# Third up projection of a transformer block pair: 19 of 22 gate/value pairs as seven products of quarter matrices, weight sums by accumulating DMAs

## The chip, the cores and the metric

One core of one Trainium2 chip. The metric is the device time of one launch in microseconds; the kernel before has 1698.54 us as the median of 3 runs (1698.29 to 1701.11). All inputs lie in device memory in float32.

## The reference

512 tokens of width 1024 go through a block with a pooling mixer and a convolutional feed-forward, then through two more blocks: forgetting attention with a SwiGLU feed-forward, and an S5 state-space mixer with a SwiGLU feed-forward. The change touches the last of these feed-forwards:

```python
D_FF_2 = 2816
def swiglu(h, w_gate, w_up, w_down):
    return (jax.nn.silu(h @ w_gate) * (h @ w_up)) @ w_down
# last lines of second_block
h = rmsnorm(x, ffn_pre_gain[i])
x = x + rmsnorm(swiglu(h, ffn_w_gate[i], ffn_w_up[i], ffn_w_down[i]), ffn_post_gain[i])
```

Here h is 512 x 1024, the two up matrices are 1024 x 2816 each, the down matrix 2816 x 1024.

## The kernel before

The stages run one after the other on TensorE: start-up and pooling, first up and down projection (`S_UP1`, `S_DN1`), attention, second up and down (`S_UP2`, `S_DN2`), S5 mixer (`S_S5I`, `S_GLU`, `S_S5O`), third up (`S_UP3`) and third down (`S_DN3`). Every float32 operand is split into a high float32r part and the rest, and a product is three passes (`passes`, L2013 to L2016): high by high, low activation by high weight, high activation by low weight.

Weights come as numbered slots through a ring of five buffers `raw`. SP issues the load of slot n when slot n - 5 is through TensorE (`ring_free`, which waits on `slot_mm`); ScalarE makes `w_hi` from it (`hi`, L806); VectorE subtracts and writes `w_lo` (`lo`, L1235); both do so three slots ahead of TensorE (`LEAD = 3`). SP, ScalarE, VectorE and GpSimd each work off their own list in order, so a wait in a list holds all that is behind it.

The third up projection has 44 slots, a gate tile and a value tile in turn. A slot is 8 blocks of 128 rows times three passes of 512 tokens. ScalarE takes Silu of the gate bank (L915), VectorE multiplies by the value bank (L1409) into `a11_s1` or `a12_a22`, and after each second pair makes the sums `s1`, `s2`, `s3`, `s4` (L1411 to L1421) that the third down projection uses: that stage is already done as seven products of quarter matrices in place of eight (`down_products`), with 11 blocks in a product and two slots' worth of banks.

The weights of that down projection need sums of quarters of `dn3`. GpSimd makes them in device memory with 32 DMAs (`weight_sums`, L1993), copies and accumulating ones, one after the other: step t waits for slot `start + t` on TensorE and for the landing of step t - 1. They start at `S_UP2 + 2`. Before them in GpSimd's list stand `s5_parameters` and the 16 `turn_tables`; each of these waits for SP's store of the one before, and SP stores them between the attention's loads (L688). After them stand the eight subtractions `hl` (L2009) that the S5 stage's gate matrix needs.

In the S5 stage ScalarE evicts a bank (`evict_u`, L1142), writes it to `u_scratch` by DMA (L1144), waits for the landing and reads it back in another order into `ub` (L1150), eight times, and only then goes on in its list; TensorE waits for `ub` at L2447.

## Time and profile before

| | |
|---|---|
| median of 3 runs | 1698.54 us |
| the profiled execution | 1701.21 us |
| its span, first to last instruction | 1699.4 us |
| granted TensorE clock, mean | 0.984 |
| TensorE busy | 1636.5 us (96%) |
| VectorE, ScalarE, GpSimd busy | 1019.0, 679.4, 267.5 us |

The profiled execution is 2.7 us above the median, and 1.8 us of it lie outside the span. TensorE's busy time counts overlapping matmuls once; the spacing of starts in its timeline tells what one costs. PEld is the load of the stationary operand, which runs beside the matmuls.

### The profile page before, as it was taken

Reading aid. Unit: us, or ns where it says so; the run is one execution under the profiler, and the core shown is the slowest. Engines: PE = TensorE matmul, PEld = TensorE weight load, DVE = VectorE, ACT = ScalarE, POOL = GpSimd, SP = SyncE. Lnnn points to the kernel's source line nnn. Section 1 sums busy time; section 2 is a strip of 40 time slices with the busy share of each in tenths; the row PEclk is TensorE's granted clock in tenths of the full one; section 3 lists DMA queues with packets and bytes.
Section 4 is the critical chain, followed back from the end, with each engine's and each line's share of the span. In section 5 each row is a group of like instructions: output and inputs, shape, how many; then the busy total and the mean of one; then the engine's idle time right before and its main releaser. Section 6 shows DMA issues by size and latency. Waiting matters only on the chain.

```text
span 1699.4 us, 21739 instructions
## 1 busy us (share of the span) xinstructions
PE 1636.5 (96%) x8385; PEld 1355.5 (80%) x8385; DVE 1019.0 (60%) x1645; ACT 679.4 (40%) x1078; POOL 267.5 (16%) x777
## 2 busy tenths in 40 slices
PE   6489999999999999999999999999999999999997
PEld 5478888888877787778888888888878888888886
DVE  6988666686554776756333337667727633333576
ACT  4455433323344767754222222333225522222564
POOL 2011700000017777730110100000010000000000
PEclk8789999999999999999999999999999999999999
DMA  8923233334342222225787763467853223232564
GB/s 351 384 76 100 87 100 99 98 126 138 98 120 84 69 76 65 85 81 169 212 197 210 211 163 126 137 191 229 261 157 125 92 98 99 100 99 88 167 190 144
DMA packets 150521, 242.30 MB, mean 143 GB/s; under 512 B 29601, under 2 KB 112913, under 8 KB 147090
## 3 DMA queue, kind: packets, MB, share of 16 engines
q1 hardware_dynamic: 130898, 210.49, 38.8%
q0 software_dynamic: 4608, 23.07, 6.0%
q10 hardware_dynamic: 14912, 7.34, 1.6%
q8 instruction: 67, 1.10, 0.3%
q14 instruction: 36, 0.29, 0.1%
HBM read 223.05 MB, written 40.89 MB: 155 GB/s over the span
## 4 chain that ended last, share of the span: by engine, by line
PE 86%; DVE 6%; DMA 4%; ACT 2%; issue 1%; POOL 0%; ACTq 0%; DVEq 0%; SPq 0%
PE bank L2014 26%; PE bank L2015 26%; PE bank L2016 26%; DVE ada L1338 2%; DMA u_scratch<-us 1%; PE bank L2328 1%; PE bank L2301 1%; PE bank L2146 1%; DVE htok L1322 1%; PE bank L2457 1%; DMA raw<-in_fox_in 1%; PE bank L2054 1%; DVE w_lo L1235 1%; ACT junk_h L874 1%; DVE xt L1298 1%
## 5 line engine op out<-in xcount | busy, mean ns | idle before, releaser
L2014 PE MATMUL bank<-hh,w_hi 128*128 128x512 f32 (+1 forms) x1440 | 552.7, 384 | 5.2 <-POOL hl L2009 3.3
L2015 PE MATMUL bank<-hl,w_hi 128*128 128x512 f32 (+1 forms) x1440 | 549.2, 381 | 0.0
L2016 PE MATMUL bank<-hh,w_lo 128*128 128x512 f32 (+1 forms) x1440 | 548.9, 381 | 0.0
L806 ACT ACTIVATE w_hi<-raw 128x1024 fp32r<-128x1024 f32 (+1 forms) x282 | 293.7, 1046 | 360.5 <-DMA raw<-in_dn 115.2
L1235 DVE TENSOR_TENSOR w_lo<-raw,w_hi 128x1024 fp32r<-128x1024 f32 (+1 forms) x282 | 335.6, 1209 | 170.2 <-ACT w_hi L806 165.9
L2014 PEld LDWEIGHTS bank<-hh,w_hi 128*128 128x128 f32 x1440 | 272.3, 189 | 58.8 <-POOL hl L2009 3.7
L2016 PEld LDWEIGHTS bank<-hh,w_lo 128*128 128x128 f32 x1440 | 272.4, 189 | 51.8
L2015 PEld LDWEIGHTS bank<-hl,w_hi 128*128 128x128 f32 x1440 | 272.6, 189 | 50.6
L2014 PE MATMUL bank<-w_hi,hid 128*128 128x512 f32 x352 | 138.2, 392 | 0.0
L2016 PE MATMUL bank<-w_hi,hid 128*128 128x512 f32 x352 | 137.1, 389 | 0.0
L2015 PE MATMUL bank<-w_lo,hid 128*128 128x512 f32 x352 | 137.0, 389 | 0.0
L915 ACT ACTIVATE scr<-bank 128x512 f32<-128x512 f32 x44 | 26.3, 598 | 246.8 <-PE bank L2016 246.8
L1396 DVE TENSOR_TENSOR scr<-scr,bank 128x512 f32<-128x512 f32 x22 | 15.1, 688 | 145.0 <-PE bank L2016 145.0
L902 ACT ACTIVATE scr<-bank,convw 128x512 f32<-128x512 f32 x44 | 34.4, 781 | 139.0 <-PE bank L2016 139.0
L2014 PEld LDWEIGHTS bank<-w_hi,hid 128*128 128x128 f32 x352 | 66.1, 188 | 15.0 <-issue 1.7
L2016 PEld LDWEIGHTS bank<-w_hi,hid 128*128 128x128 f32 x352 | 66.1, 188 | 13.8
L2015 PEld LDWEIGHTS bank<-w_lo,hid 128*128 128x128 f32 x352 | 66.1, 188 | 13.3
L1851 POOL TENSOR_TENSOR turn_new<-turn_t 128x2 f32<-128x2 f32 (+2 forms) x192 | 71.4, 372 | 15.0
L1371 DVE SCALAR_TENSOR_TENSOR scr<-bank,convw,scr 128x511 f32<-128x511 f32 x44 | 33.0, 749 | 64.4 <-ACT scr L902 64.4
L2014 PE MATMUL bank<-w_hi,a_hi 128*128 128x512 f32 x154 | 60.4, 392 | 0.8 <-DVE w_lo L1235 0.8
L2015 PE MATMUL bank<-w_lo,a_hi 128*128 128x512 f32 x154 | 60.0, 389 | 0.0
L1409 DVE TENSOR_TENSOR a_a<-scr,bank 128x512 f32<-128x512 f32 x11 | 7.6, 688 | 87.2 <-PE bank L2016 87.2
(324 smaller groups left out, 2184.3 us busy)
## 6 DMA issues: line engine op xcount, KB each, us to landing
raw<-in_up SPq DMA_DIRECT2D x132, 512.0 KB, 3.3
raw<-in_dn SPq DMA_DIRECT2D x55, 512.0 KB, 4.2
ada<-in_ada_w SPq DMA_DIRECT2D x24, 1024.0 KB, 8.6
v_scratch<-in_dn POOLq DMA_DIRECT2D x24, 704.0 KB, 6.4
raw<-in_fox_in SPq DMA_DIRECT2D x32, 512.0 KB, 3.7
raw<-in_s_w SPq DMA_DIRECT2D x24, 512.0 KB, 3.8
raw<-v_scratch SPq DMA_DIRECT2D x20, 512.0 KB, 3.8
v_scratch<-v_scratch POOLq DMA_DIRECT2D x8, 704.0 KB, 5.1
```

Of the source, the lines that this page charges most:

```text
L806: act.activation(w_hi[:, n % RING, 0:w], raw[:, n % RING, 0:w], ACT.Copy).then_inc(hi_done, 1)
L874: own.add(act.activation(junk_h[:, :], xt[:, b, :], ACT.Square, scale=1 / 32, accum_out=ss_x[:, b:b + 1]))
L902: act.activation(scr[:, 2 * s, :], bank[base + (2 * j + s) % 4][:, :], ACT.Identity, scale=convw[:, j, 4 * s + 1:4 * s + 2], bias=convw[:, ...
L915: act.activation(scr[:, j % 2, :], bank[base + (2 * j) % 4][:, :], ACT.Silu).then_inc(act_done, 1)
L1235: dve.tensor_tensor(w_lo[:, n % RING, 0:w], raw[:, n % RING, 0:w], w_hi[:, n % RING, 0:w].bitcast(F32), ALU.subtract).then_inc(lo_done, 1)
L1298: own.add(dve.scalar_tensor_tensor(xt[:, b, 0:HALF], ya[:, b, :], rn1[:, b:b + 1], xt[:, b, 0:HALF], ALU.mult, ALU.add))
L1338: dot = dve.tensor_tensor_reduce(wt, wt, csil[:, :], 1.0, 0.0, ALU.mult, ALU.add, accum_out=dots[:, m, 2 * b + t:2 * b + t + 1])
L1371: own.add(dve.scalar_tensor_tensor(c[:, 1:T], b[:, 0:T - 1], convw[:, j, 4 * s:4 * s + 1], c[:, 1:T], ALU.mult, ALU.add))
L1851: own.add(pool.tensor_tensor(out_, a, b, op))
L2014: pe.matmul(dst, w_h, r_h, start=first, stop=False, skip_group_check=True)
L2015: pe.matmul(dst, w_h, r_l, start=False, stop=False, skip_group_check=True)
L2016: return pe.matmul(dst, w_l, r_h, start=False, stop=last, skip_group_check=True)
```

## The change

Three of the 22 pairs (`PLAIN`) stay as they were. For each of the other 19 the product of the 256 + 256 tokens by 512 + 512 inputs of h with the gate and value tiles (each 1024 x 128, cut into two halves of 512 inputs) is done as a 2 x 2 by 2 x 2 block product with seven quarter products of 4 blocks by 256 tokens instead of eight. A pair is now four slots: gate low half and v2, v4 and v1, gate high half and v3, value high half (a half slot). Loads of the first and third of them are two DMAs of 256 KB each. v1 to v4 are sums of the gate and value halves, made in device memory by GpSimd. The banks of successive pairs alternate between 0 to 3 and 4 to 7.

VectorE forms four sums of quarters of h (`h_combinations`) during the plain pairs, and ScalarE and VectorE split them. In each pair ScalarE copies the first product, VectorE forms the four results by five operations on 256 columns, ScalarE takes Silu in two halves. The sums `s3` and `s4` of the hidden values move from the up stage to the first product of the down stage, since their place is taken by the sums of h. The 32 sums for the down projection start at `S_UP1 + 22` in place of `S_UP2 + 2` and ahead of the turn tables; 56 new DMAs (`up_sums`) start at `S_UP2 + 2`. They move 768 or 512 KB each, in rows of 2 KB where the old ones have rows of 5.5 KB. SP waits for the last of them ahead of the first pair's load.

```diff
+PLAIN = 3
+PAIRED = HT - PLAIN
+S_PAIRS = S_UP3 + 2 * PLAIN
+S_DN3 = S_PAIRS + 4 * PAIRED
+SUM_CHUNKS = ((2, 5), (5, 8), (8, 11), (12, 15), (15, 18), (18, 20), (20, 22))
...
+            sp.wait_ge(sum_step, 16 * (DOWN_SUMS + 8 * len(SUM_CHUNKS)))
+            for p in range(PAIRED):
+                n, j = S_PAIRS + 4 * p, last_up_tile(PLAIN + p)
+                load_halves(n, dram["up3"][2 * j, :, 0:T], v2_v3[0, j])
+                load_fm(n + 1, v4_v1[j].rearrange("p t c -> p (t c)"))
+                load_halves(n + 2, dram["up3"][2 * j, :, T:D], v2_v3[1, j])
+                load_halves(n + 3, dram["up3"][2 * j + 1, :, T:D])
...
+                for p in range(PAIRED):
+                    n, x = S_PAIRS + 4 * p, pair_banks(p)[0]
+                    before = HT * (f - 1) + PLAIN + p
+                    act.wait_ge(pair_mm, 3 * p + 1)
+                    act.wait_ge(y_step, 4 * p - 3) if p else act.wait_ge(val_done, before)
+                    act.activation(g_p1, x[:, 0:QN], ACT.Copy).then_inc(p1_done, 1)
...
+                    hi(n + LEAD)
+                    hi(n + 1 + LEAD)
+                    hi(n + 2 + LEAD)
+                    act.wait_ge(pair_mm, 3 * p + 3)
+                    act.wait_ge(val_done, before)
+                    act.activation(g_gate[:, 0:QN], x[:, 0:QN], ACT.Silu)
+                    act.wait_ge(y_step, 4 * p + 4)
+                    act.activation(g_gate[:, QN:T], g_c21, ACT.Silu).then_inc(act_done, 1)
+                    hi(n + 3 + LEAD)
...
+                for p in range(PAIRED):
+                    n, j = S_PAIRS + 4 * p, PLAIN + p
+                    x, y, w, z = pair_banks(p)
+                    lo(n + LEAD)
+                    dve.wait_ge(p1_done, p + 1)
+                    dve.wait_ge(slot_mm, n + 1)
+                    dve.tensor_tensor(g_u2, y[:, 0:QN], g_p1, ALU.add).then_inc(y_step, 1)
+                    lo(n + 1 + LEAD)
+                    dve.wait_ge(pair_mm, 3 * p + 2)
+                    dve.wait_ge(y_step, 4 * p + 1)
+                    dve.tensor_tensor(g_u3, w[:, 0:QN], g_u2, ALU.add).then_inc(y_step, 1)
...
+                    dve.tensor_tensor(g_val[:, QN:T], z[:, 0:QN], g_u3, ALU.subtract).then_inc(y_step, 1)
+                    lo(n + 2 + LEAD)
+                    dve.wait_ge(slot_mm, n + 3)
+                    dve.tensor_tensor(g_c21, y[:, 0:QN], g_u3, ALU.add).then_inc(y_step, 1)
+                    dve.wait_ge(slot_mm, n + 4)
+                    tt(g_val[:, 0:QN], z[:, 0:QN], g_u2, ALU.subtract)
...
+                    dve.tensor_tensor(hid_quarters(j), g_gate, g_val, ALU.mult).then_inc(val_done, 1)
+                    lo(n + 3 + LEAD)
                     if j % 2:
+                        hid_combinations(j, f)
...
                 def split_lo(i, c):
                     k0, k1 = A_CHUNKS[c]
+                    if i == 1:
+                        own.add(dve.scalar_tensor_tensor(s3[:, k0:k1, :], s2[:, k0:k1, :], -1.0, a12_a22[:, k0:k1, 1, :],
+                                                         ALU.mult, ALU.subtract))
+                        own.add(dve.tensor_tensor(s4[:, k0:k1, :], a12_a22[:, k0:k1, 0, :], s2[:, k0:k1, :], ALU.add))
+                        own.settle()
...
+            def up_sums(start):
...
+                steps = ((v4, val[:, :, lo_k], False), (v1, gate[:, :, lo_k], False), (v4, val[:, :, hi_k], True),
+                         (v1, val[:, :, lo_k], True), (v2_v3[0], v1, False), (v2_v3[0], val[:, :, hi_k], True),
+                         (v2_v3[1], v2_v3[0], False), (v2_v3[1], gate[:, :, hi_k], True))
+                for t, ((to, src, add), (j0, j1)) in enumerate(itertools.product(steps, SUM_CHUNKS)):
+                    pool.wait_ge(slot_mm, start + t + 1)
+                    pool.wait_ge(sum_step, 16 * (DOWN_SUMS + t))
...
+            weight_sums(S_UP1 + 22)
+            for k in range(PAIRS // 2):
+                turn_tables(k)
+            up_sums(S_UP2 + 2)
...
+                def product(n, half, dst, a, first_, last):
+                    s = n % RING
+                    for k in range(KH):
+                        w = slice(T * half + P * k, T * half + P * k + P)
+                        mm = passes(dst, w_hi[:, s, w], w_lo[:, s, w], a[0][:, k, :], a[1][:, k, :],
+                                    first_ and k == 0, last and k == KH - 1)
+                    return mm
...
+                    product(n, 0, x, a11, True, False).then_inc(pair_mm, 1)
...
+                    product(n, 1, y, m2, True, True).then_inc(slot_mm, 1)
...
+                    product(n + 1, 0, w, m3, True, True).then_inc(pair_mm, 1)
...
+                    product(n + 1, 1, z, m1, True, False).then_inc(slot_mm, 1)
+                    pe.wait_ge(lo_done, n + 3)
+                    pe.wait_ge(p1_done, p + 1)
+                    product(n + 2, 0, x, a12, False, True).then_inc(pair_mm, 1)
+                    pe.wait_ge(y_step, 4 * p + 1)
+                    product(n + 2, 1, y, a22, True, True).then_inc(slot_mm, 1)
+                    pe.wait_ge(lo_done, n + 4)
+                    pe.wait_ge(y_step, 4 * p + 3)
...
+                    product(n + 3, 0, z, m4, False, True).then_inc(slot_mm, 1)
```

## Rows read from the trace of the kernel before

**Rows 1.** The page: busy time by engine.

```profile
PE 1636.5 (96%) x8385; PEld 1355.5 (80%) x8385; DVE 1019.0 (60%) x1645; ACT 679.4 (40%) x1078; POOL 267.5 (16%) x777
```

**Rows 2.** The page: the chain that ended last, by engine.

```profile
PE 86%; DVE 6%; DMA 4%; ACT 2%; issue 1%; POOL 0%; ACTq 0%; DVEq 0%; SPq 0%
```

**Rows 3.** Busy time by stretch; last three columns granted clock, DMA share, GB/s.

```profile
96.00:340.00 244.00, 243.04 (x1114) 202.59 (x1113) 171.32 (x233) 102.48 (x133) 43.19 (x112) 1.00 0.30 97
...
780.00:1020.00 240.00, 239.99 (x1091) 199.92 (x1090) 92.61 (x115) 60.92 (x70) 21.90 (x32) 1.00 0.73 198
1020.00:1155.00 135.00, 134.70 (x731) 112.20 (x730) 92.24 (x129) 45.40 (x77) 0.00 (x0) 1.00 0.54 157
1155.00:1340.00 185.00, 176.75 (x1270) 149.71 (x1269) 114.80 (x213) 65.43 (x98) 10.28 (x8) 0.98 0.60 175
1352.00:1581.00 229.00, 229.00 (x1015) 189.79 (x1014) 85.45 (x123) 55.82 (x64) 0.00 (x0) 1.00 0.31 100
```

**Rows 4.** TensorE timeline (start, duration): 256-column passes, 55 between these two.

```profile
1345.73 0.28 PE L2014 MATMUL bank<-hh,w_hi 128*128 128x256 f32 x1
...
1352.44 0.28 PE L2016 MATMUL bank<-hh,w_lo 128*128 128x256 f32 x1
```

**Rows 5.** TensorE timeline: first pass of one 24-pass slot and of the next.

```profile
1445.07 0.39 PE L2014 MATMUL bank<-hh,w_hi 128*128 128x512 f32 x1
...
1450.51 0.39 PE L2014 MATMUL bank<-hh,w_hi 128*128 128x512 f32 x1
```

**Rows 6.** VectorE groups of 1352 to 1581: count, busy us, mean ns, idle before.

```profile
L1235 DVE TENSOR_TENSOR w_lo<-raw,w_hi 128x1024 fp32r<-128x1024 f32 x42 | 49.5, 1221 | 1.5
L1239 DVE TENSOR_TENSOR s<-a_s 128x256 f32<-128x256 f32 x20 | 8.4, 422 | 0.3
...
L1409 DVE TENSOR_TENSOR a_a<-scr,bank 128x512 f32<-128x512 f32 x10 | 6.9, 688 | 79.2 <-PE bank L2016 79.2
```

**Rows 7.** ScalarE groups of 1352 to 1581.

```profile
L806 ACT ACTIVATE w_hi<-raw 128x1024 fp32r<-128x1024 f32 x43 | 45.4, 1057 | 39.8 <-DMA raw<-in_up 35.4 <-DMA raw<-in_dn 4.3
L915 ACT ACTIVATE scr<-bank 128x512 f32<-128x512 f32 x21 | 12.6, 598 | 133.5 <-PE bank L2016 133.5
```

**Rows 8.** ScalarE timeline after the slot that ends at 1445.07.

```profile
1445.27 0.60 ACT L915 ACTIVATE scr<-bank 128x512 f32<-128x512 f32 x1 [6.22 <-PE bank L2016]
...
1448.62 1.06 ACT L806 ACTIVATE w_hi<-raw 128x1024 fp32r<-128x1024 f32 x1 [1.81 <-DMA raw<-in_up]
```

**Rows 9.** DMA issues, KB, us to landing: 1352-1575, then 790-1005.

```profile
raw<-in_up SPq DMA_DIRECT2D x38, 512.0 KB, 3.2
...
raw<-in_up SPq DMA_DIRECT2D x37, 512.0 KB, 4.1
```

**Rows 10.** The sums: issue duration ns, first and last start.

```profile
L2002 POOL DMA_DIRECT2D v_scratch<-in_dn x16: 800/812/949, 840.0 to 996.3; - x16
L2005 POOL DMA_DIRECT2D v_scratch<-in_dn x8: 517/517/811, 793.9 to 834.9; - x8
```

**Rows 11.** Line L1144, ScalarE's writes to u_scratch: who waited, and landing times.

```profile
L1144 ACTq DMA_DIRECT2D u_scratch<-us x8: 332/336/350, 1162.2 to 1218.4; - x8
...
  ACT us L1142: 17.0, 4
...
DMA to landing us min/median/max: 3.9/6.0/8.5
```

**Rows 12.** GpSimd timeline: the second turn table, and the first hl.

```profile
502.46 0.10 POOL L1916 MEMSET turn_new<- 128x2 f32 x1 [296.94 <-DMA turn_scratch<-turn_new]
...
1219.53 2.67 POOL L2009 TENSOR_TENSOR hl<-yfm,hh 128x512 fp32r<-128x512 f32 x2 [222.38 <-ACT hh L1160]
```

**Rows 13.** TensorE timeline: passes after its wait for hl.

```profile
1241.54 0.80 PE L2014 MATMUL bank<-hh,w_hi 128*128 128x512 f32 x1 [3.31 <-POOL hl L2009]
1242.13 0.63 PE L2015 MATMUL bank<-hl,w_hi 128*128 128x512 f32 x1
1242.56 0.63 PE L2016 MATMUL bank<-hh,w_lo 128*128 128x512 f32 x1
```

More of the change, by code:

```diff
@@ L291, in build, with h_quarter @@
         of_s = in_hid("of_s", [KT, T], F32, EAT)
+        KH = KT // 2
+        h_parts = in_hid("h_parts", [4, KH, QN], F32, FAT + 3 * T)
+        COMBS = G3AT
+        m2_hi, m2_lo, m3_hi, m3_lo, m1_hi = (in_hid(name, [KH, QN], F32R, COMBS + t * KH * QN) for t, name in
+                                             enumerate(("m2_hi", "m2_lo", "m3_hi", "m3_lo", "m1_hi")))
+        m1_lo = at("m1_lo", [KH, QN], F32R, gpre_at)
+        def h_quarter(part, k_half, t_half):
+            return part[:, KH * k_half:KH * k_half + KH, QN * t_half:QN * t_half + QN]
+        M_HI = (m2_hi[:, :, :], m3_hi[:, :, :], m1_hi[:, :, :], h_quarter(hh, 0, 1))
+        M_LO = (m2_lo[:, :, :], m3_lo[:, :, :], m1_lo[:, :, :], h_quarter(hl, 0, 1))
+        M_RAW = tuple(h_parts[:, t] for t in (0, 1, 3, 2))
+        g_p1, g_u2, g_u3, g_c21 = scr[:, 0, 0:QN], scr[:, 0, QN:T], scr[:, 1, 0:QN], scr[:, 1, QN:T]
+        g_val, g_gate = scr[:, 2, :], scr[:, 3, :]
         A_RAW = [a11_s1[:, :, 0, :], s2[:, :, :], s3[:, :, :], a11_s1[:, :, 1, :], a12_a22[:, :, 1, :], s4[:, :, :],
@@ L540, in by_place, with pair_banks @@
             return y.rearrange("p (s j) -> p s j", s=BLK)
-        BX, BY, BW, BZ = (4, 5), (6, 7), (0, 1), (2, 3)
+        BX, BY, BW, BZ = (0, 1), (2, 3), (4, 5), (6, 7)
+        def pair_banks(p):
+            first = 0 if p % 2 else 4
+            return bank[first:first + 4]
         PROD_BANK = (BX, BY, BW, BZ, BY, BZ, BX)
@@ L916, in silu_up, with split_h_hi, silu_up_pairs @@
                     hi(n + 1 + LEAD)
+            def split_h_hi(i):
+                act.wait_ge(comb_done, i + 1)
+                if i == 3:
+                    act.wait_ge(slot_mm, S_PAIRS)
+                act.activation(M_HI[i], M_RAW[i], ACT.Copy).then_inc(a_hi_done, 1)
+            def silu_up_pairs(first, f, base):
+                for j in range(PLAIN):
+                    n = first + 2 * j
+                    hi(n + LEAD)
+                    if j == 1:
+                        split_h_hi(0)
+                    if j == 2:
+                        split_h_hi(1)
+                    act.wait_ge(slot_mm, n + 1)
+                    if j >= 2:
+                        act.wait_ge(val_done, HT * (f - 1) + j - 1)
+                    act.activation(scr[:, j % 2, :], bank[base + (2 * j) % 4][:, :], ACT.Silu).then_inc(act_done, 1)
+                    if j == 2:
+                        split_h_hi(2)
+                    hi(n + 1 + LEAD)
[5 more added lines that the diff above has]
+                    act.activation(g_p1, x[:, 0:QN], ACT.Copy).then_inc(p1_done, 1)
+                    if p == 0:
+                        split_h_hi(3)
+                    hi(n + LEAD)
+                    hi(n + 1 + LEAD)
+                    hi(n + 2 + LEAD)
[5 more added lines that the diff above has]
+                    hi(n + 3 + LEAD)
             def store_tables(i, b0):
@@ L1400, in silu_up, with h_combinations, whole @@
                     lo(n + 1 + LEAD)
-            def silu_up_quarters(first, f, base):
-                for j in range(HT):
-                    n, k = first + 2 * j, j // 2
-                    lo(n + LEAD)
+            def h_combinations():
+                part = lambda t: h_parts[:, t]
+                def whole(t, k_half, t_half):
+                    tt(part(t), h_quarter(hh, k_half, t_half).bitcast(F32), h_quarter(hl, k_half, t_half).bitcast(F32), ALU.add)
+                dve.wait_ge(hl_done, 8 * LAST)
+                whole(1, 0, 1)
+                whole(3, 1, 1)
+                yield
+                tt(part(3), part(1), part(3), ALU.subtract)
+                whole(0, 0, 0)
+                yield
+                tt(part(1), part(0), part(1), ALU.subtract)
+                tt(part(0), part(3), part(0), ALU.subtract)
+                dve.sem_inc(comb_done, 3)
+                yield
+                whole(2, 1, 0)
+                tt(part(2), part(2), part(0), ALU.add)
+                dve.sem_inc(comb_done, 1)
+                yield
@@ L1406, in silu_up_quarters, with silu_up_pairs @@
+            def silu_up_pairs(first, f, base):
+                combinations = h_combinations()
+                for j in range(PLAIN):
+                    n = first + 2 * j
+                    lo(n + LEAD)
+                    if j < 2:
+                        next(combinations)
+                    if j == 0:
+                        next(combinations)
+                    if j == 2:
+                        split_h_lo(0)
+                        split_h_lo(1)
                     dve.wait_ge(act_done, HT * f + j + 1)
@@ L1990, in _ @@
             s5_parameters()
-            for k in range(PAIRS // 2):
-                turn_tables(k)
             def weight_sums(start):
```

172 lines of the change are left out of this document (117 added, 55 removed).

## Prediction, made before the changed kernel was run

> **What bounds the kernel now.** I read the page's busy times first: TensorE is busy 96% of the span [rows 1], and it carries 86% of the chain that ended last [rows 2]. The stretches then show that this holds stage by stage: in the third up projection, 1352 to 1581, TensorE is busy all 229 us, VectorE 85 and ScalarE 56 [rows 3]. ScalarE and VectorE sit idle there until a bank is through [rows 6, 7]. So only TensorE's own work counts in this stage, until another engine's list or a load grows past it. The S5 stage, 1155 to 1340, is the one in which TensorE idles: 185 less 176.8, some 8 us [rows 3].
>
> **What the seven products save.** A 512-column pass costs 226.7 ns: one slot of 24 takes 1450.51 - 1445.07 = 5.44 us [rows 5]. For 256 columns the count of columns would halve it to 113, but the boundary ahead of this stage shows the very form: 56 steps in 1352.44 - 1345.73 = 6.71 us, 120 ns each, with the weight tile as stationary operand and a new one for every pass [rows 4]. A pair was 48 passes of 226.7 ns, 10.88 us. It becomes 7 products x 4 blocks x 3 passes = 84 passes of 120 ns, 10.08 us. That is 0.80 us a pair, and 19 pairs give **15.2 us**. By columns alone it would be an eighth of 207 us, 26 us; the cost of the short pass takes 11 of them.
>
> The Trainium skill ("TensorE: Matmul & The Clock Gate", LDWEIGHTS) gives a weight load as 128 / 1.2 = 107 ns, and says ("The mechanism") that it overlaps matmuls only where the row group differs. By that a 256-column pass would cost 107 for the load and 107 for its columns, 84 of them 17.9 us, an estimate from the page. The row contradicts it: 120 ns with loads for every pass.
>
> **Whether the other engines keep up in a pair of 10.08 us.** VectorE does three full `lo` (3 x 1.22) and a half one (0.69 as the 512-wide form), five operations on 256 columns (5 x 0.42), one on 512 (0.69), and every second pair five operations of at most 0.42 for the hidden sums, 1.05 a pair [rows 6]: together 8.2 us. ScalarE does 3 x 1.06 + 0.6, and three of 256 columns that I put at 0.37 each from the difference between its 1024 and 512 forms [rows 7]: 4.9 us. Both fit on the sum, but they are now linked with TensorE four times a pair. The tightest loop: the pair's first slot's buffer comes free when the slot before the pair ends; from there to the start of `hi` it takes 1448.62 - 1445.07 = 3.55 us [rows 5, 8]. Behind that stand a second DMA issue for the two-part load (some 0.35), `hi` 1.06, `lo` 1.22, and, since VectorE's list is in order, `g_u3` and the first half of `g_val`, 0.42 each: 7.0 us. TensorE needs that `g_val` before its seventh product, 6 x 1.44 = 8.64 us in. Slack **1.6 us**, less some tenths for semaphores. A load took 3.2 us here and 4.1 with other DMAs beside it [rows 9]; SP now moves 1.75 MB in 10.1 us in place of 1 MB in 10.9, still less than the 198 GB/s of the stretch with the sums [rows 3]. I take no stall: 0, with an upper bound of 0.4 us a pair (8 us in all) if landings grow to 5.3.
>
> The sums of h are 8 operations of 1024 elements and 4 splits, 12 x 1.22 = 15 us [rows 6], in three plain pairs of 10.88 us in which VectorE needs some 10: 25 of 32 us, hidden. Taking `s3` and `s4` out of the up stage gains nothing, as VectorE idles there.
>
> **What it costs in the down stage.** There `s3` and `s4` come in VectorE's list between the `lo` of slots 4 to 6 of the first product, whose TensorE time is 66 passes x 226.7 = 15.0 us. From the end of the last pair VectorE has 0.4 + 0.7 + 1.2 + 2 = 4.3 us left over, then `lo` 1.2, then three turns of a `lo`, the two sums and a split, 1.2 + 2.4 + 1.2 = 4.8 us each with the last of them shorter after its `lo`. The `lo` of the second product's first slot ends at about 4.3 + 1.2 + 4.8 + 4.3 + 1.2 = 15.8, and that of the next at about 20 against a need at 18.5. So TensorE waits 1 to 2.6 us in the second product; I take **+1.7 us**.
>
> **The sums by DMA.** The old 32 took 996.3 - 793.9 = 202.4 us for 31 steps, 6.53 us each [rows 10], which is more than a slot's 5.44, so the chain of landings sets their pace. TensorE did not wait in that stretch (239.99 of 240 us [rows 3]) though loads took 4.1 in place of 3.2 us [rows 9]. Moved to the first up stage, they meet a DMA share of 0.30 [rows 3]; the slot they wait for ends near 226 (340, where that stage ends, less 21 slots of 5.44), they need 209 us and end about 435, and GpSimd had 297 us of idle time before 502 there [rows 12], with only one turn table to make. Cost 0.
>
> The 56 new steps start at 794 as the old ones did. To 1020 they do 35 at the old pace. The other 21 run through the second down stage, whose DMA share is already 0.54 [rows 3]; I put them at 7.4. That gives about 1175. The rows are 384 instead of 128 a step, and GpSimd's issue (0.52 and 0.81 us [rows 10]) could grow with them: between 0 and +1.3 us a step, I take 0.5, nearer to unchanged, since the step's time is mostly the data and its landing. Last issue then about **1200** (1153 at the old pace throughout, over 1236 at the upper bound). In the S5 stage they meet ScalarE's writes to `u_scratch`: these begin at 1162 and ScalarE waits 17 us for four of them, at 3.9 to 8.5 us each [rows 11]. That chain is where TensorE idles. From the loads' +0.9 and from the spread 3.9 to 6.0 I put each of five writes at +1.2: **+6 us** (0 if the sums end by 1160; 13 at 5 x 2.6, or with a drop of the clock).
>
> The Trainium skill ("DMA: Bandwidth & Descriptors", Anatomy of one DMA) has 2.0 us + bytes / 436 GB/s for a DMA from GpSimd, an estimate of 3.8 us for 768 KB. By it the sums would go at TensorE's slot pace, and end before 1115. The 6.53 of the rows is far above, so I give it little.
>
> **Sum.** -15.2 + 1.7 + 6 = -7.5 us. On the profiled execution, 1701.2 - 7.5 = 1693.7; that execution lay 2.7 above the median, so 1691.0 for the median of runs.
>
> **Rivals.**
> 1. *The sums do not touch S5.* They end by 1165, or the round of packets lets the small ones through. For it: the rows' old pace. Against it: a DMA share of 0.54 + 0.43 in the second down stage. 1698.5 - 13.5 = 1685.
> 2. *The pair's loop binds.* Landings of 5.3 us, or dearer short operations, make a pair 10.4: 0.33 x 19 = 6 on top, 1697. For it: the 4.1 [rows 9] and four links a pair; against it: no sums run in that stage, and 1.6 us of slack.
> 3. *Slower: GpSimd reaches `hl` late.* The `hl` subtractions stand behind the 56 sums in its list. The first ran at 1219.5 [rows 12] and TensorE waited for the second pair of them until 1241.5 [rows 13]. Two pairs take 5.2 us, so the last issue must come before 1236: (1236 - 794) / 55 = 8.05 us a step. From there each us is a us of the end; the gain of 13.5 is gone at about 8.3. At 8.5 the last issue is at 1261: 25 us late, 1698.5 - 13.5 + 25 = 1710. For it: three times the rows, 6.5 + 1.3 is 7.8 before contention. Against it: most of a step is data.
> 4. *Weight loads come to bound the short passes.* In the up stage TensorE's loads are busy 189.8 us for 1014, 187 ns each [rows 3], longer than a 256-column pass. If they don't hide here, a pass costs up to the 226.7 ns of the long one, the nearest row above: 19 x (84 x 0.2267 - 10.88) = 155 us slower, 1854. Against it: the 120 ns [rows 4]. (The page's overlap rule above would lead here.)
> 5. *TensorE's clock.* After TensorE's 3.3 us wait for `hl` the passes come 0.43 us apart in place of 0.227 [rows 13], so half of 2.4 GHz, for about 6 us, some 2.7 lost. Each S5 or pair stall that grows to such a length adds this. Two or three of them and a larger S5 slip: 1698 to 1701.
>
> **How the numbers follow.** Forecast (1687 to 1696): 0.45. Rival 1: 0.22. Rival 2: 0.10. Rival 3: 0.12. Rival 4: 0.01. Rival 5: 0.10. A measurement of this kernel tells about 0.2%, 3.4 us, from no change, so faster ends at 1695.1 and slower begins at 1701.9. Faster: 0.43 + 0.22 + 0.03 from rival 2 + 0.01 = 0.69. Same: 0.02 + 0.05 + 0.02 from rival 3 + 0.07 = 0.16. Slower: 0.02 + 0.10 + 0.01 + 0.02 = 0.15. The range runs from the bare saving, 1698.5 - 15.2 = 1683, to 1701, where rivals 2 and 5 end; rival 3's bulk and rival 4 are left out.
>
> **What the profile will show.** 1596 passes of the third up stage at 128x256, starts 120 ns apart, a pair every 10.08 us; if pairs come further apart, the wait ahead of the seventh product names `g_val` (rival 2) or `w_lo`. A wait of 1 to 3 us for `w_lo` in the second down product. The sums' last issue between 1170 and 1230, and landings of `u_scratch` over 6 us in the median with more TensorE idle time than 8 us in the S5 stretch; if that is unchanged, rival 1. GpSimd's `hl` starting right behind a DMA issue shows rival 3. I am wrong if a 256-column pass with float32r operands from the new places costs other than 120 ns, or if the first down stage, where sums and tables now meet, makes TensorE wait.

## The result and the profile after

The changed kernel takes 1719.6 us in the median of four runs (1710.8 to 1724.7), against 1699.0 for the kernel before (1698.3 to 1701.1). The ratio is 1.0114, with a 95% interval of 1.0071 to 1.0157: some 19 us slower, where 8 us faster was forecast. The profiled execution took 1720.28 us with a span of 1718.2.

Two lines of the page of after, busy time by engine and then the chain that ended last, answer [rows 1, 2]:

```profile
PE 1629.2 (95%) x9069; PEld 1379.5 (80%) x9069; DVE 1102.5 (64%) x1774; ACT 724.7 (42%) x1158; POOL 319.5 (19%) x833
...
PE 74%; DVE 11%; DMA 8%; ACT 3%; issue 2%; SPq 0%; POOL 0%; ACTq 0%; DVEq 0%
```

TensorE is busy 7 us less than before, in a span that is 19 us longer. Its share of the chain fell from 86% to 74%, and VectorE and DMA took what it lost. So other stages paid for what the third feed-forward gained; the stretches show which. Busy time by stretch of after, cut at the same TensorE operations as in [rows 3] (last three columns granted clock, DMA share, GB/s):

```profile
96.00:340.00 244.00, 243.35 (x1117) 202.85 (x1116) 171.27 (x234) 102.76 (x133) 44.15 (x90) 1.00 0.50 149
340.00:469.00 129.00, 121.50 (x633) 99.14 (x631) 78.92 (x107) 34.05 (x54) 24.18 (x54) 0.97 0.74 200
789.00:1029.00 240.00, 240.00 (x1090) 200.09 (x1091) 92.86 (x114) 60.94 (x70) 31.41 (x34) 1.00 0.73 200
1029.00:1177.00 148.00, 139.30 (x732) 115.00 (x730) 91.83 (x128) 44.86 (x77) 17.89 (x19) 0.97 0.88 234
1177.00:1371.00 194.00, 177.85 (x1264) 150.78 (x1265) 114.53 (x213) 65.79 (x98) 15.14 (x12) 0.96 0.67 181
1383.00:1597.00 214.00, 214.00 (x1700) 210.24 (x1699) 160.58 (x245) 99.97 (x143) 0.00 (x0) 1.00 0.52 175
```

What to see: TensorE idles in three of them, the first down stage (129 less 121.5), the second down stage (148 less 139.3) and the S5 stage (194 less 177.9), and in each the granted clock is below 1. The first and second up projection bear GpSimd's transfers too, at a DMA share of 0.50 and 0.73, and TensorE idles there for 0.65 us (0.96 before) and not at all; in the third it is busy all the time.

Set side by side by the start of the same TensorE instruction in both traces, after is this many us behind before. The same was read for each experiment below (e1d to e11), and the table holds them all, so that each can be judged stage by stage. Each row is one profiled execution. Differences of a few tenths to 1 us at the start come from the start-up. All kernels built from after except e8 also gain some 2 us between 420 and 520: there TensorE's wait for `htok`, ahead of the attention, is 0.9 to 1.1 us, where before has 1.7 us and then a granted clock of 0.50 from 480 to 483.

| us behind the trace of before, at | 364, first tables | 520, attention | 1044, second tables | 1139, end of second down | 1202, S5's first scans | 1327, end of S5 | 1665, last transposes |
|---|---|---|---|---|---|---|---|
| after | 1.3 | 8.4 | 8.6 | 15.7 | 32.0 | 31.0 | 18.9 |
| e1d | -0.5 | -2.7 | -2.3 | -2.3 | -3.7 | -4.6 | -16.8 |
| e2d | 0.6 | 7.9 | 8.3 | 21.2 | 37.6 | 38.9 | 39.1 |
| e3d | 0.4 | 9.7 | 9.6 | 9.6 | 8.5 | 10.5 | 10.5 |
| e4d | 0.2 | -2.2 | 7.4 | 7.4 | 8.9 | 9.0 | -3.7 |
| e5 | 0.7 | -1.3 | -2.1 | -2.1 | -0.9 | -0.3 | 0.3 |
| e6 | 1.0 | 2.5 | 2.3 | 7.2 | 6.2 | 7.0 | -5.5 |
| e7 | 0.5 | 1.3 | 7.3 | 7.3 | 6.3 | 5.9 | -6.5 |
| e8 | 0.7 | 0.6 | 0.4 | 0.4 | -0.2 | -1.2 | -13.7 |
| e9 | -0.3 | -3.0 | -3.5 | -3.5 | -4.4 | -4.5 | -13.7 |
| e10 | 0.2 | 0.0 | -0.8 | 6.2 | 6.0 | 7.2 | -5.0 |
| e11 | 0.8 | -1.3 | -1.8 | -1.8 | 16.8 | 20.2 | 7.9 |

After thus is 7 us further behind at 520 than at 364 (by 420 it was 9, 10.4 less 1.3, all in the first down stage, and 2 came back ahead of the attention). It loses 7 more in the second down stage and 15 between there and the end of S5, and gets 12 back in the third feed-forward.

The gain is where it was expected. TensorE's timeline of after, first pass of the first pair and first pass of the third down stage; 19 pairs lie between them:

```profile
1405.36 0.28 PE L2194 MATMUL bank<-hh,w_hi 128*128 128x256 f32 x1
...
1596.87 0.40 PE L2194 MATMUL bank<-w_hi,a_hi 128*128 128x512 f32 x1
```

1596.87 - 1405.36 = 191.51 us, 10.08 for each pair, 120 ns for each pass.

The losses name their releasers. TensorE's waits of after, first of 340 to 560 and then of 1100 to 1380 (total, times, longest):

```profile
PE bank L2370 <- DVE ya L1344: 5.9, 1, 5.9
...
PE bank L2676 <- DMA ub<-u_scratch: 10.7, 2, 8.8
PE bank L2370 <- DVE ya L1344: 4.2, 1, 4.2
PE bank L2194 <- DVE w_lo L1323: 3.4, 1, 3.4
```

L2370 is the transpose of a table in a down stage, `ya` at L1344 VectorE's eviction that its bank waits for. VectorE's list is in order, so what made it late is further back. The chain of waits of after ending at 421.8 (start, duration):

```profile
392.36 9.13 DMA raw<-in_dn
...
404.53 0.96 ACT w_hi L853
405.51 0.06 DVE w_lo L1323
...
406.66 1.16 DVE r_tab L1672
...
419.19 2.47 DVE ya L1344 x4
421.80 1.94 PE bank L2370 x8
```

A load of 512 KB took 9.1 us. `w_hi`, `w_lo`, then the table and then the eviction stand behind it in lists. DMA issues of 340 to 440 (KB, median us to landing), after and then before:

```profile
raw<-in_dn SPq DMA_DIRECT2D x12, 512.0 KB, 8.9
...
raw<-in_dn SPq DMA_DIRECT2D x15, 512.0 KB, 5.5
```

The wait is followed by passes at a lower clock. Stretches of 7 and 6 us of after, up to and behind its end:

```profile
415.00:422.00 7.00, 1.14 (x6) 0.67 (x5) 6.75 (x13) 0.00 (x0) 0.82 (x1) 0.79 0.63 110
422.00:428.00 6.00, 6.00 (x46) 4.66 (x46) 0.86 (x1) 0.00 (x0) 0.81 (x1) 0.68 1.05 250
```

TensorE was idle for 5.9 us, then the granted clock was 0.68 in the mean over 6 us in which it never idled, that is, some of it at 1.2 GHz and the rest at 2.4: 6 x (1 - 0.68), another 1.9 us. From 428 to 434 it was 1.00 again. The wait for `ub` at 1200.8 (8.8 us) shows the same, with 0.74 in the 6 us behind it.

### The profile page after: what moved, and what is told of

It is laid out like the page before. It is cut to its first block, busy times and chain, and to the rows that moved or that the text cites. A ratio compares the mean times of both kernels' runs of the same rounds, so it can differ in the third digit from the quotient of the medians.

```text
span 1718.2 us, 23609 instructions
## 1 busy us (share of the span) xinstructions
PE 1629.2 (95%) x9069; PEld 1379.5 (80%) x9069; DVE 1102.5 (64%) x1774; ACT 724.7 (42%) x1158; POOL 319.5 (19%) x833
## 3 DMA queue, kind: packets, MB, share of 16 engines
q0 software_dynamic: 20096, 62.92, 16.6%
## 4 chain that ended last, share of the span: by engine, by line
PE 74%; DVE 11%; DMA 8%; ACT 3%; issue 2%; SPq 0%; POOL 0%; ACTq 0%; DVEq 0%
PE bank L2194 23%; PE bank L2196 22%; PE bank L2195 22%; DMA raw<-in_dn 3%; DMA u_scratch<-us 2%; DVE ada L1426 2%; DVE w_lo L1323 1%; PE bank L2557 1%; DMA cc<-in_s_c 1%; PE bank L2530 1%; DVE prod L1673 1%; DVE r_tab L1675 1%; DVE r_tab L1672 1%; ACT w_hi L853 1%; PE bank L2686 1%
## 5 line engine op out<-in xcount | busy, mean ns | idle before, releaser
L2194 PE MATMUL bank<-hh,w_hi 128*128 128x512 f32 (+1 forms) x1440 | 521.1, 362 | 7.3 <-DVE w_lo L1323 3.4
L2195 PE MATMUL bank<-hl,w_hi 128*128 128x512 f32 (+1 forms) x1440 | 517.4, 359 | 0.0
L2196 PE MATMUL bank<-hh,w_lo 128*128 128x512 f32 (+1 forms) x1440 | 517.0, 359 | 0.0
L1323 DVE TENSOR_TENSOR w_lo<-raw,w_hi 128x1024 fp32r<-128x1024 f32 x320 | 373.5, 1179 | 210.8 <-ACT w_hi L853 205.7
L853 ACT ACTIVATE w_hi<-raw 128x1024 fp32r<-128x1024 f32 x320 | 325.3, 1021 | 415.4 <-DMA raw<-in_dn 175.4
L2179 POOL DMA_DIRECT2D v_v_scratch<-in_up x28 | 33.7, 1203 | 211.1 <-DMA v_v_scratch<-in_up 190.6
L2013 POOL TENSOR_TENSOR turn_new<-turn_t 128x2 f32<-128x2 f32 (+2 forms) x192 | 64.5, 336 | 15.0
L2194 PE MATMUL bank<-m_hi,w_hi 128*128 128x256 f32 x228 | 64.5, 283 | 0.0
L2195 PE MATMUL bank<-m_lo,w_hi 128*128 128x256 f32 x228 | 64.5, 283 | 0.0
L2196 PE MATMUL bank<-m_hi,w_lo 128*128 128x256 f32 x228 | 64.5, 283 | 0.0
```

Source lines behind the costliest of these rows:

```text
L853: act.activation(w_hi[:, n % RING, 0:w], raw[:, n % RING, 0:w], ACT.Copy).then_inc(hi_done, 1)
L1323: dve.tensor_tensor(w_lo[:, n % RING, 0:w], raw[:, n % RING, 0:w], w_hi[:, n % RING, 0:w].bitcast(F32), ALU.subtract).then_inc(lo_done, 1)
L2013: own.add(pool.tensor_tensor(out_, a, b, op))
L2179: pool.dma_start(dst, src, accum_op=ALU.add).then_inc(sum_step, 16)
L2194: pe.matmul(dst, w_h, r_h, start=first, stop=False, skip_group_check=True)
L2195: pe.matmul(dst, w_h, r_l, start=False, stop=False, skip_group_check=True)
```

## Experiments

All kernels differ from before or from after by the diff that is shown. Medians are given with the ratio to the kernel before and its 95% interval.

**The pairs without the sums (e1d).**

```diff
-            weight_sums(S_UP1 + 22)
             for k in range(PAIRS // 2):
                 turn_tables(k)
-            up_sums(S_UP2 + 2)
+            weight_sums(S_UP2 + 2)
...
-                load_fm(n + 1, v4_v1[j].rearrange("p t c -> p (t c)"))
+                load_fm(n + 1, dram["up3"][2 * j + 1])
```

> This kernel is the changed one without the 56 steps that sum quarters of the up weights (the pairs load plain weight rows of the same size and row length in their place, so its third up projection does not compute the reference's), and with the 32 steps for the down weights back where the kernel before has them. Theory (the products save what was forecast, and all of the loss is the sums' transfers meeting other stages): 1699.0 - 15.2 + 3.0 (second and first down product, as the trace of after shows) = 1686.8 us, pairs 10.08 us apart, nothing added before 1352. Rival (the products or the new memory places cost something of their own beside the sums): over 1692 us.

Measured: 1687.5 us, ratio 0.9940 (0.9923 to 0.9957), that is -10.2 us (-7.3 to -13.1). By the table it gains 12.2 between 1327 and 1665. So the products bring what the trace of after shows, 15.2 less the 3 us of the down stage. With the 56 new sum transfers gone and the old 32 back at their place, no loss is left. This kernel does not read the new arrays of sums in device memory; that reading them costs nothing is shown by after and e8, which do, and whose pairs come 10.08 us apart as well.

**The sums without the pairs (e2d).** The kernel before with the GpSimd list of after (the definition of `up_sums`, the same as in after, is left out here):

```diff
+            weight_sums(S_UP1 + 22)
             for k in range(PAIRS // 2):
                 turn_tables(k)
-            weight_sums(S_UP2 + 2)
+            up_sums(S_UP2 + 2)
```

> The kernel before, third up projection unchanged, but with GpSimd's whole new list: 32 steps in the first up and down stage, 56 from the second up projection on, whose results nobody reads. Theory (contention alone makes the loss): 1699.0 + 31 = 1730 us, with a spread of some 10 us from run to run as after has it. Rival (the loss needs the pairs, or lies in code order): within 5 us of 1699.

Measured: 1736.0 us (1728.5 to 1740.5), ratio 1.0201 (1.017 to 1.0231), +34 us. Nothing was changed but when the old sums are made and that new ones, which nobody reads, are made too. So the loss needs no pairs: transfers beside other stages make it. With e1d, 34 - 10 = 24 us stand against the 19 of after, within their intervals.

**The old 32 steps moved alone (e3d).** The kernel before with `weight_sums(S_UP1 + 22)` ahead of the turn tables, where `weight_sums(S_UP2 + 2)` had stood behind them.

> The kernel before with one edit: the 32 steps for the down weights start in the first up projection, ahead of the turn tables. Theory (they meet the first down stage's loads and tables): 1699.0 + 8.5 = 1707.5 us, the loads of the first down stage at 8 us in the median in place of 5.5, a wait of some 6 us before the tables' transposes. Rival (cost 0, as the prediction had it; the slip in after comes from elsewhere): 1699 us.

Measured: 1704.3 us (1700.3 to 1711.6), ratio 1.0035 (1.0017 to 1.0052), +5.9 us. The profiled execution was one of the long ones, 9.7 behind before at 520. TensorE's waits of e3d in 340 to 480:

```profile
PE bank L2015 <- ACT kt L928: 5.8, 1, 5.8
PE bank L2142 <- DVE ya L1256: 2.7, 1, 2.7
```

The first down stage pays, though in two places and not one: the second wait, at 455.7, is ahead of its last products. Its 512 KB loads took 6.6 us in the median from 340 to 440, where before had 5.5 and after 8.9. The ten runs spread over 11 us. Cost 0 is refuted.

**The same 88 steps at other times (e4d).** Against after:

```diff
-            weight_sums(S_UP1 + 22)
-            for k in range(PAIRS // 2):
+            sum_steps(20)
+            turn_tables(0)
+            sum_steps(7, S_DN1 + DNS - 1)
+            for k in range(1, PAIRS // 2):
                 turn_tables(k)
-            up_sums(S_UP2 + 2)
+                sum_steps(1)
+            sum_steps(DOWN_SUMS + 8 * len(SUM_CHUNKS) - 54, S_FO + 6)
```

`sum_steps(n, slot)` issues the next n steps, each after the landing of the one before and, where a slot is named, not before TensorE is through that slot. 12 more stand between the operations of `s5_parameters`.

> The changed kernel with the same 88 steps at other times: 12 among GpSimd's S5 parameters and 20 behind them in the first up projection, none in the first down stage, 7 in the value projection, one behind each turn table, the rest from the end of the attention output on. Theory (it is the down and S5 stages that cannot bear the sums, not their bytes): the last issue comes before 1040, nothing slips in the S5 stage, 1687 to 1690 us, faster than both kernels. Rival (the sums cost by their bytes wherever they run): 1710 to 1720 us. Rival (GpSimd's turn tables come late by the added issues, and SyncE's loads wait for them): a loss of 5 us or more in the attention stage.

Measured: 1697.9 us, ratio 0.9994 (0.9981 to 1.0006), 20 us less than after with the same bytes. The table shows why: nothing is lost in either down stage, 1.6 us in S5. So the bytes do not cost the same wherever they run. The theory fell short by some 9 us, though, and its last rival was right too: +5.4 near 550 and +4.5 near 760. TensorE's waits of e4d in 500 to 800:

```profile
PE bank L2520 <- DVE qk L1798: 5.4, 1, 5.4
PE bank L2210 <- DVE w_lo L1323: 3.2, 1, 3.2
```

The first of them goes back to SyncE. Chain of waits of e4d ending at 548.6:

```profile
539.22 0.33 POOL turn_new L2013
539.61 0.52 SPq L723
540.17 4.01 DMA raw<-in_fox_in
544.21 1.06 ACT w_hi L853
545.33 1.14 issue
546.47 0.75 DVE qf L1793
```

SP's store of the turn table (L723) waits for GpSimd, and a weight load stands behind that store. Sum issues at 504.6 and 509.1 had made GpSimd late, and the load went out at 540.2 where before it went at 537.2.

**Sums in the up stages alone (e5).** The up sums come first; 32 steps in the first up projection, 5 at 470, 33 from 786, and the last 18 from `S_UP3 + 1`:

```diff
...
+            sum_steps(5, S_DN1 + DNS - 1)
+            for k in range(1, PAIRS // 2):
+                turn_tables(k)
+            sum_steps(33, S_UP2 + 2)
...
+            sum_steps(UP_SUMS + DOWN_SUMS - 70, S_UP3 + 1)
```

> The changed kernel with the steps for the up weights first and those for the down weights last: 32 in the first up projection, 5 in the value projection, 33 in the second up projection, and the last 18 (down weights) in the third up projection itself; none beside the turn tables, the down stages and S5. Theory (an up projection bears them, the stages with bursts of loads and tables do not): 1686 to 1689 us, that is the 1687.5 of the kernel without the up sums, and the 5.8 us wait before the query's product and the 3.6 us wait in the attention output of the run with steps beside the turn tables are gone. Rival (the pair loop with its 1.6 us of slack cannot bear them): pairs come 10.2 to 10.5 us apart while the 18 steps run, 1690 to 1694 us. Rival (bytes cost wherever they run): no better than 1698.

Measured: 1701.9 us, ratio 1.0015 (1.0001 to 1.003). Up to 1327 the kernel is level with before, as the theory has it, and then the 12 us of the third feed-forward do not come: 0.7 us for each of 18 steps. While these run, to 1477, pairs come 10.1 to 14.0 us apart, and all nine pairs behind them at 10.08. The first rival holds, at more than the size that was written down. TensorE's waits of e5 in 1383 to 1500, and the loads (KB, median us to landing), of e5 in 1383 to 1480 and then of after in 1383 to 1580:

```profile
PE bank L2211 <- DVE scr L1568: 6.0, 6, 2.4
PE bank L2211 <- DVE scr L1559: 2.1, 4, 0.8
PE bank L2211 <- DVE w_lo L1324: 1.8, 1, 1.8
```

```profile
raw<-v_v_scratch SPq DMA_DIRECT2D x9, 512.0 KB, 6.9
raw<-v_v_scratch SPq DMA_DIRECT2D x17, 256.0 KB, 5.0
```

```profile
raw<-v_v_scratch SPq DMA_DIRECT2D x19, 512.0 KB, 3.3
raw<-v_v_scratch SPq DMA_DIRECT2D x37, 256.0 KB, 3.5
```

L1568 is the subtraction that makes the second half of `g_val`. With landings of 3.3 to 3.5 us the pair loop has slack, with 5 to 7 it binds. This was rival 2 of the prediction, brought about by transfers that after does not have in this stage.

**Copies in place of accumulating transfers (e6).** Both `accum_op=ALU.add` of the sums taken out (16 of the 32 old steps and 28 of the 56 new ones; the 20 in the expectation was miscounted).

> The changed kernel with each accumulating transfer of the sums (20 of the 32, 28 of the 56) made a plain copy of the same source; the sums are then not formed, so the output is not the reference's. Theory (the accumulating steps are the long ones, 8 to 14 us against 5 to 7, because they also read their destination): the 56 steps end near 1120 in place of 1208, S5 slips by under 3 us instead of 9 to 15, the whole is 1695 to 1702 us. Rival (what hurts is that GpSimd's queue is active at all beside the loads' queue): the slips stay, 1712 us or more.

Measured: 1695.5 us, ratio 0.9971 (0.9959 to 0.9983), 24 us less than after. The last step is issued at 1109 in place of 1208. The GpSimd queue of the page, after and then e6 (packets, MB, share of 16 engines):

```profile
q0 software_dynamic: 20096, 62.92, 16.6%
```

```profile
q0 software_dynamic: 15232, 62.92, 11.2%
```

The table shows what is left: the second down stage still loses 5 us, S5 nothing; its steps have ended before S5 begins. The first down stage loses 3.7 us by 420, with a wait of 1.9 us for `ya`.

**Fewer and larger steps (e7).** From e4d. The counts in GpSimd's list, left out here, change with it: 22 steps in the first up projection, 4 in the value projection, 22 in the second up projection, and none beside the turn tables.

```diff
-SUM_CHUNKS = ((2, 5), (5, 8), (8, 11), (12, 15), (15, 18), (18, 20), (20, 22))
+SUM_CHUNKS = ((2, 7), (7, 11), (12, 17), (17, 22))
-itertools.product(steps, range(4))
+itertools.product(steps, (slice(0, 2), slice(2, 4)))
```

> The changed kernel with the same sums in fewer and larger steps: 16 of 1408 KB for the down weights and 32 of 1024 or 1280 KB for the up weights in place of 32 and 56; 22 in the first up projection, 4 in the value projection, 22 in the second up projection, none elsewhere. From the rows of the runs so far a copying step takes 3.5 us and 0.8 us for each tile, an accumulating one 3.9 and 1.7, so the 32 steps take 309 us in place of 398. Theory (the loss is only the overlap with the down, attention and S5 stages, and the sums are rid of it once they fit into the three others): the last issue before 1020 us, 1687 to 1690 us, faster than both kernels by some 10 us, no slip of more than 2 us ahead of the third up projection. Rival (larger steps hold the engines longer, and the up projections' loads come late): waits in the first or second up projection, 1693 us or more.

Measured: 1693.9 us, ratio 0.9971 (0.9958 to 0.9984). Faster than before, by half of what was expected. Size and places were changed together, so the gain over e4d is that of both. The last of the 48 steps is issued at 1018. Three slips of 2 to 4 us are left, each near a step or a turn table at the edge of the two up projections or outside them. TensorE's waits of e7 in 340 to 1340:

```profile
PE bank L2518 <- DVE qk L1798: 3.0, 1, 3.0
PE bank L2384 <- DVE ya L1344: 2.2, 1, 2.2
...
PE bank L2208 <- DVE w_lo L1323: 1.8, 1, 1.8
```

The first is the attention stage's, where the step issued at 502.7 made the second turn table late. The second is the first down stage's, where the first turn table now ran beside the tables; that it is the cause is not shown. The run e10 below has this table back at its old place, and yet waits 2.1 us at the same operation, behind a load of 6.9 us with no sum beside it. The last comes at 1038, behind a load of 11.4 us (`cc`) that went out at 1021.5, some 3 us after the last step.

**The three slips taken out (e8).**

```diff
-            sum_steps(14)
             turn_tables(0)
-            sum_steps(4, S_DN1 + DNS - 1)
+            sum_steps(13)
+            sum_steps(3, S_DN1 + DNS - 1)
             for k in range(1, PAIRS // 2):
                 turn_tables(k)
+                if k in (4, 6, 8, 10, 12):
+                    sum_steps(1)
-            sum_steps(DOWN_SUMS + 8 * len(SUM_CHUNKS) - 26, S_UP2 + 1)
+            sum_steps(DOWN_SUMS + 8 * len(SUM_CHUNKS) - 29, S_UP2 + 1)
```

> The run with fewer and larger steps, its three remaining slips treated one by one: the first turn table stands at its old place ahead of the sums and not beside the first down stage's tables (that run was 2.9 us late there, with a wait of 2.5 before the tables' transposes), 3 instead of 4 steps in the value projection (its fourth made the second turn table late; 3.4 us wait before the query's product), and 5 steps behind turn tables 4 to 12, so that the last comes near 1000 and not at 1018 (2.2 us wait at 1038). Theory: those 7 us come back, 1687 to 1689 us, ratio 0.993 to 0.995. Rival (the slips belong to any load of this size and only move): 1692 us or more.

Measured: 1688.7 us (1687.7 to 1690.1), ratio 0.9931 (0.9917 to 0.9944), 11.7 us less than the kernel before and some 31 less than after. It is the version that beats both. It moves the same 62.92 MB through GpSimd's queue as after does (16.2% of the engines' time against 16.6%). Against e1d, which forms no up sums at all, it is 1.2 us longer by the medians. The three edits were made together, so what each gave is read only from the table: against e7, 6 of the 7 us come between 520 and 1044, from the second and third edit. The 1 us ahead of 520 is within what executions differ by there: e8, e9 and e10 have the same list up to 890 and stand 1.0, -0.3 and 2.5 us behind before at 420.

**s4 on GpSimd (e9).** From e8, `s4` by `pool.tensor_tensor`, with a wait of VectorE for it ahead of the split that overwrites `s2`.

> The same as the run before it, with one more edit in the last down stage: GpSimd computes the sum s4, three operations of 1024 or 768 elements, and VectorE keeps s3 alone. Theory (the 1.6 and 1.4 us that TensorE waits in the second product are VectorE's list being 3.6 us of sums too long): both waits fall below 0.3 us, 3 us less than the run before it. Rival (the waits come from ScalarE's copies or from GpSimd being slower at the same work, which VectorE now waits for): the waits stay or grow.

Measured: 1690.5 us, ratio 0.9940 (0.9923 to 0.9957), not to be told from e8 by the medians. TensorE's waits in the down stage grow from 2.0 to 3.6 us, the rival's side, and by the starts of the same TensorE instructions e9 loses 6.0 us between 1581 and 1665, where e8 loses 2.7. e8 and then e9, TensorE's waits of 1570 to 1600, and GpSimd's group of 1560 to 1640:

```profile
PE bank L2210 <- DVE w_lo L1323: 2.0, 2, 1.1
```

```profile
PE bank L2217 <- DVE w_lo L1326: 3.6, 2, 2.0
...
L2212 POOL TENSOR_TENSOR s<-a_a,s 128x1024 f32<-128x1024 f32 (+1 forms) x3 | 9.6, 3226 | 303.0 <-DVEq L1532 303.0
```

The group mixes two shapes: 3.4 us for an operation of 1024 elements, where VectorE needs 1.2, and 2.8 for the one of 768. VectorE waits for it.

**The price of a step, stage by stage (e10, e11).** From e8, the last 8 steps moved into the second down stage, or the last 6 to the head of S5:

```diff
-            sum_steps(DOWN_SUMS + 8 * len(SUM_CHUNKS) - 29, S_UP2 + 1)
+            sum_steps(11, S_UP2 + 1)
+            sum_steps(8, S_DN2 + 1)
```

```diff
+            sum_steps(13, S_UP2 + 1)
+            sum_steps(6, S_S5I - 2)
```

> The fitted kernel (all sums in the quiet stages) with its last 8 steps, four copying and four accumulating ones of 1024 or 1280 KB, moved from the second up projection into the second down stage. Theory (the down stage has no room for them: its loads go out in bursts of three, between its tables, and its lists wait for the last of a burst): 3 to 7 us later than the fitted kernel by 1155 us of the trace, 1692 to 1696. Rival (most of what after lost in that stretch was S5's first loads, and the down stage alone bears the steps): under 1 us later at 1155.

Measured: 1697.1 us, ratio 0.9984 (0.9973 to 0.9994), 9 us over e8, just above the range; by the table 7 us are lost between 1044 and 1139, so the rival (under 1 us) is out. Loads issued at 1092 took up to 13.6 us.

> The fitted kernel with its last 6 steps, two copying and four accumulating ones, moved to the boundary ahead of the S5 stage and its first scans. Theory (that stage's own small transfers wait behind them, one after another): landings of u_scratch writes and reads over 7 us where they were 4 to 6, a wait of 5 us or more ahead of the products with ub, 6 to 13 us later than the fitted kernel at the end of the stage, 1695 to 1702. Rival (the S5 stage lost its 9 us in after only because it began with the down stage's delay): under 2 us.

Measured: 1709.0 us, ratio 1.0058 (1.0042 to 1.0074), 21.6 us over e8, more than the 13 at the upper end. Its second down stage ends 1.8 us ahead of before, and S5 still ends 20.2 behind, so no delay carried over from the down stage is needed. Of the lines on the tile `u_scratch`, who waited for it, e8 and then e11 (us, times):

```profile
  ACT us L1230: 11.6, 3
...
  PE bank L2692: 1.7, 2
```

```profile
  PE bank L2693: 13.2, 3
  ACT us L1230: 12.0, 2
```

So a step of 1.0 to 1.25 MB costs nothing to speak of in the first two up projections, some 1.1 us in the down stage (9 / 8), and 3.6 us in S5 (21.6 / 6). These are prices of these two mixes, four copying and four accumulating steps there and two and four here.

## Why the prediction was wrong

**What bounds the kernel.** Right. In the third up stage TensorE alone counts, and it stays busy 214 of 214 us with VectorE at 160.6 and ScalarE at 100.

**What the seven products save.** Right to the digit: 120 ns a pass, 10.08 us a pair, 15.2 us in all. Weight loads are busy 210 us of the 214 and no pass waits for one, so rival 4 is gone. The overlap rule of the Trainium skill ("TensorE: Matmul & The Clock Gate", "The mechanism"), by which the pairs would have cost more than before, does not hold for these passes. (The section also names a second condition, a background weight buffer; no run here tells by which of them these loads overlap.)

**The pair loop.** Right for after: no stall, 0 us. That the slack is small is shown by e5, where landings of 5 to 7 us make it bind, most of it at the wait that was named (`g_val` ahead of the seventh product, 6.0 us of the waits above).

**The sums of h, s3 and s4.** The cover of the first held. For the second +1.7 was taken, out of 1 to 2.6; the stage takes 3.05 us more (18.85 behind at its end, 1596.87 - 1581.07 = 15.8 at its start). The mechanism was right, VectorE's list, and so were the times: the `lo` of the two slots end 16.4 and 20.3 us into the stage, where 15.8 and about 20 had been reckoned. TensorE waits for both of them, gaps of 1.68 and 1.35 us with 0.23 as the usual one, so the upper end was due and not a value between; passes behind a gap then start 0.33 us apart for once. The term was short by 1.3.

**"Moved to the first up stage, they meet a DMA share of 0.30 ... Cost 0."** This step failed, and it is the first cause of the miss. The working itself had the sums end about 435 (the last is issued at 437.5), and thus put nearly half of them beyond 340, into the first down stage. Of that stage it looked at GpSimd's idle time and not at the loads. "TensorE did not wait in that stretch", the evidence that sums are free, is a row of an up projection, where a load goes out each 5.4 us. A down stage sends its loads out in groups of three or four between tables, and ScalarE's and VectorE's lists wait for the last of a group while tables and evictions stand behind it. 5.5 us to landing before became 8.9, and 9 us were lost by 420; e3d, which changes nothing else, measures +5.9 (2.9 to 8.8) on the whole time. The closing sentence named this as what would make the prediction wrong, and no rival carried it.

**The second down stage** got a pace of 7.4 us for the 21 steps in it, but no price at all. It lost 7 us: the same step, left out. Even the plain copies of e6 lose 5 there, and 8 steps in e10 lose 7.

**The pace of the sums.** The end was right, 1207.7 against "about 1200", and so was the mean: 405 us for 55 steps, 7.4 each, from a start that lay 8.6 us later than reckoned. The parts were not: copies 5.9 us and accumulates 8.9, in place of one rate of 6.5 to 7.4 (and 0.5 on top) for all, so that the mean came out is partly luck. That the two kinds differ stood in the rows of the old steps, which issue in 812 ns where they accumulate and in 517 where they copy [rows 10], and was not followed up. The rule of the Trainium skill ("DMA: Bandwidth & Descriptors", Anatomy of one DMA), an estimate of 3.8 us for such a transfer, is below both.

**The S5 stage, "+6 us (0 ... 13)".** The place and the mechanism were right, the term was mis-sized: 15 us in after, 17.7 in e2d from 1139 to 1327. It was built from five writes at +1.2 each, and +1.2 is what the median write took more (7.2 us against 6.0 of [rows 11]). But ScalarE waited 2.5 us more for each of four, 27.0 us in all against 17.0. In the trace of after the line of the writes, what waited for the tile `u_scratch`, and the landings of its writes and reads together:

```profile
L1232 ACTq DMA_DIRECT2D u_scratch<-us x8: 332/335/347, 1184.3 to 1250.4; - x8
...
  ACT us L1230: 27.0, 4
...
  PE bank L2676: 10.7, 2
...
DMA to landing us min/median/max: 2.7/7.2/10.4
```

A round trip is a write and a read, so each turn pays twice. And 4.5 of the 15 us are lost before this chain begins, between 1139 and 1155 of the trace of before: the first S5 weight load was late, and no term stood for it. The chain of waits of after has it, and the longest write:

```profile
1160.75 10.12 DMA raw<-in_s_w
...
1191.36 10.00 DMA u_scratch<-us
```

All transfers issued between 1146 and 1170 took 8 to 12 us to landing. The long wait for `ub` is then followed by passes at a lower clock.

**The rivals.** Rival 3's threshold for `hl` was not reached: the last sum is issued at 1207.7, the first `hl` starts at 1251.6, and each time GpSimd had waited for ScalarE's `hh`; TensorE's wait for it is 2.0 us in after, less than the 3.3 before. Rival 5, the clock after stalls, did happen and adds up to 2 us a time, on the far side of the range. None of them explains 1719.6: where they have the sums cost something, it is in S5 or in GpSimd's list, and the forecast had one term for contention where there were three.

## What to carry to other kernels

Price a background transfer by the stage it runs in, by asking who waits for a landing there and how many landings follow one another, not by the DMA share or by a stretch where it happened to be free. The same 63 MB made after 32 us longer than e1d and e8 1 us longer, by when they ran and in how many steps; find the stages where each load has a slot's time to spare, count how many steps fit, and make the steps larger and fewer until they do. How steady a stage is without them counts too: the same first down stage differed by up to 2.8 us between executions of one list (e9, e10). Before an issue is put on an engine's list, look at which other queue waits for that list, as SyncE waited for GpSimd's turn tables here.
